# Expert stage with 88 token places instead of 96, and two of sixteen weight blocks as whole 128-column products

## The chip, the cores and the metric

One Trainium2 chip; the kernel runs on one of its cores. The metric is the device time of one execution in microseconds, given as the median of several runs.

## What is computed

The reference is two transformer blocks on 256 tokens of width 1024, all in float32. The part that the change touches is the mixture of experts of the first block's second layer:

```python
def moe_swiglu(h, w_router, w_gate, w_up, w_down):      # h: 256 x 1024
    logits = (h @ w_router).astype(jnp.float32)
    top_val, top_idx = lax.top_k(logits, TOP_K)          # 2 of 8 experts a token
    top_w = jax.nn.softmax(top_val, axis=-1)
    gates = jnp.sum(jax.nn.one_hot(top_idx, N_EXPERTS, dtype=jnp.float32) * top_w[..., None], axis=-2)
    out = jnp.zeros_like(h)
    for e in range(N_EXPERTS):
        y = swiglu(h, w_gate[e], w_up[e], w_down[e])     # 1024 -> 3584 -> 1024
        out = out + gates[..., e:e + 1].astype(h.dtype) * y
    return out
```

Before it stand a gated linear attention, a dense feed forward and a stick-breaking attention; behind it the second block with a gated delta net, convolutional feed forwards and latent attention. None of these is changed.

## The kernel before

**Weights** come as 547 tiles of 1 MiB (128 partitions x 2048 numbers) in the order of their use. SP loads them into `ring`, seven slots; `load_turns` (L160) waits on `tile_used` until the tile seven places earlier has been used, then issues the next transfer. TensorE waits on `landed` of the slot before a tile and adds one to `tile_used` with the tile's last product. All stages share this one stream.

**Routing** (L1195 to L1302). The router's products, top two, softmax; a rank for each token within its expert; `pick`, a 0/1 matrix that gives each chosen token its place among the CAP places of its expert; `place`, which carries gates back to tokens. `flag` (L1254) is set if an expert has more than CAP tokens; then a second path (from L1475), guarded by an If on each engine, computes the experts again for the tokens beyond. It is not entered otherwise.

**Expert stage** (L1304 to L1443), one core, experts in turn. Each expert has 28 gate/up tiles (`nf`) and 14 down tiles (two halves of `kd` = 7), 42 in all, 336 for eight experts. On TensorE, written out by hand in this order:
- for each gate/up tile `s`: wait for the tile, for `moe_hid` (the buffer of two tiles earlier is free), then 2 halves x 8 `k`, each block of 128x128 weights as two products with 64 weight columns, `m` = 0 and 64, that write partitions 0 to 63 and 64 to 127 of the same PSUM columns (L1368). The weights are the stationary side, the expert's CAP tokens (`hTe`) are streamed.
- behind tile 1, `turn` (L1330): eight transposes of the expert before; behind tile 5, `spread_rows` (L1337): four products of 512 columns that add its result to the tokens.
- behind the 28th, `gather` (L1311) of the next expert's tokens: 8 x 2 products, each again as two strips (L1316).
- then the down tiles: 4 `j` x 4 `q` blocks a tile, each as two strips (L1390), CAP tokens of `hid` streamed.

ScalarE takes the silu of each gate/up tile (L1406) when its products are done, VectorE multiplies it with the up half (L1418) into `hid`; VectorE also copies tokens, turned rows and sums. GpSimd copies one 256-wide row set an expert. In float32 one `nc.tensor.matmul` of the program appears in the trace as two pairs of LDWEIGHTS and MATMUL instructions. The page prints L1368 and L1390 for the strip products, L352 and L2316 for products of other stages that are 128 columns wide.

Other lines that the prediction speaks of: L552 and L568 are products of an early stage, L2057, L2061, L2097, L2127 and L2130 of the gated delta net in the second block.

Of the kernel before, what the change touches and what calls it, by code (L numbers as in the profile page):

```python
# [19 lines left out]
P = 128  # L20
D = 1024
KT = D // P
# [10 lines left out]
F_FFN = 2816 // P  # L33
FF = 2816
EPS = 1e-6
CAP = 96
GH = 4
MH = 8
LANES = 4
# [24 lines left out]
def build(nc, stream, params, where, out):  # L64
# [4 lines left out]
    with ExitStack() as ctx:  # L69
# [15 lines left out]
        ps = ctx.enter_context(nc.psum_tensor("ps", [P, 8, 512], F32))  # L85
# [14 lines left out]
        def after_all(eng):  # L100


            for d in everyone:
                n = d.n if len(chain) == 1 else chain[-1].get(d, 0)

                if n and not (len(chain) > 1 and eng.engine == nc.tensor.engine and d in (tile_used, pe_done)):
                    eng.wait_ge(d.sem, n)
# [13 lines left out]
        def link(eng, done, ins):  # L121

            eng.wait_ge(done.sem, done.by(ins))
# [10 lines left out]
        def take(*shape):  # L134
            n = int(np.prod(shape))
            assert cur[0] + n <= ARENA, (cur[0], n)
            v = arena[:, cur[0]:cur[0] + n]
            cur[0] += n
            if len(shape) == 2:
                v = v.rearrange("p (a b) -> p a b", a=shape[0])  # L140
            if len(shape) == 3:
                v = v.rearrange("p (a b c) -> p a b c", a=shape[0], b=shape[1])
            return v
# [5 lines left out]
        @block.sync  # L149
        def _(sp):  # L150

            first = where["first"]
            sp.dma_start(par[:, 0:first], params[:, 0:first]).then_inc(params_in, 16)
            for t in range(RING):
                sp.dma_start(ring[:, t, :], stream[t]).then_inc(landed[t], 16)
            sp.dma_start(par[:, first:width], params[:, first:width]).then_inc(rest_in, 16)
            for t in range(TT):
                sp.dma_start(cx[:, t, :], out["ctx"][t * P:t * P + P, :]).then_inc(rest_in, 16)
# [1013 lines left out]
        finish()  # L1172
        hid = take(F_MOE, CAP)
        sg = take(2, CAP)
        hTe = take(KT, CAP)
        pick = take(TT, EXPERTS, P)
        place = take(EXPERTS + 1, SEQ)
        placed = take(SEQ)
        yT = take(KT, CAP)
        y = take(D)  # L1180
# [69 lines left out]
        def _(dve):  # L1250
            after_all(dve)
            nc.vector.tensor_reduce(over[:, 0:1], ps[:, 4, 16:24], AXX, ALU.max)
            link(dve, dve_done, nc.vector.tensor_copy(rank.rearrange("p t n -> p (t n)"), ps[:, 4, 0:16]))
            link(dve, dve_done, nc.vector.tensor_scalar(flag, over[:, 0:1], float(CAP), None, ALU.is_gt))  # L1254

            link(dve, dve_done, nc.vector.tensor_scalar(rest, rank, float(CAP), None, ALU.is_ge))
            link(dve, dve_done, nc.vector.tensor_tensor(rest, rest, gates, ALU.mult))
# [50 lines left out]
        slot = lambda k: (moe_t0 + k) % RING  # L1308
        wait_of = lambda k: 16 * ((moe_t0 + k) // RING + 1)

        def gather(pe, e):  # L1311

            for k in range(KT):
                for t in range(TT):
                    for m in (0, 64):
                        last = nc.tensor.matmul(ps[m:m + 64, 4 + k // 4, (k % 4) * P:(k % 4) * P + CAP],  # L1316
                                                xn[:, t, k * P + m:k * P + m + 64], pick[:, t, e, 0:CAP],
                                                start=(t == 0), stop=(t == TT - 1), skip_group_check=True)
            last.then_inc(moe_gathered, 1)
# [10 lines left out]
        def turn(pe, e):  # L1330

            pe.wait_ge(moe_sums, e * 2 + 2)
            for k in range(KT):
                last = nc.tensor.transpose(ps[0:CAP, 6 + k // 4, (k % 4) * P:(k % 4) * P + P], yT[:, k, :], ident)
            last.then_inc(moe_turned, 1)

        def spread_rows(pe, e):  # L1337

            pe.wait_ge(moe_y, e + 1)
            pe.wait_ge(moe_place, e + 1)  # L1340
            for half in range(2):
                for t in range(TT):
                    last = nc.tensor.matmul(ps[:, 2 * t + half, :], placed[0:CAP, t * P:t * P + P],
                                            y[0:CAP, half * 512:half * 512 + 512], start=False, stop=False,
                                            skip_group_check=True)
            last.then_inc(moe_spread, 1)
# [5 lines left out]
        @block.tensor  # L1352
        def _(pe):
            after_all(pe)
            gather(pe, 0)
            for e in range(EXPERTS):
                at = e * per

                pe.wait_ge(moe_tokens, e + 1)
                for s in range(nf):  # L1360
                    pe.wait_ge(landed[slot(at + s)], wait_of(at + s))
                    w = ring[:, slot(at + s), :].rearrange("p (k n) -> p k n", k=KT)

                    pe.wait_ge(moe_hid, e * nf + s + 1)
                    for half in range(2):
                        for k in range(KT):
                            for m in (0, 64):
                                last = nc.tensor.matmul(ps[m:m + 64, 4 + s % 2, half * P:half * P + CAP],  # L1368
                                                        w[:, k, half * P + m:half * P + m + 64], hTe[:, k, :],
                                                        start=(k == 0), stop=(k == KT - 1), skip_group_check=True)  # L1370
                    last.then_inc(tile_used.sem, 1)

                    if s == TURN_AT:
                        turn(pe, e)
                    if s == SPREAD_AT:
                        spread_rows(pe, e)

                pe.wait_ge(moe_hid, e * nf + (nf + 2))
                if e + 1 < EXPERTS:
                    gather(pe, e + 1)  # L1380

                for half in range(2):
                    for d in range(kd):
                        k0 = at + nf + half * kd + d
                        pe.wait_ge(landed[slot(k0)], wait_of(k0))
                        w = ring[:, slot(k0), :].rearrange("p (k n) -> p k n", k=4)
                        for j in range(4):
                            for q in range(4):
                                for m in (0, 64):
                                    last = nc.tensor.matmul(ps[m:m + 64, 6 + half, q * P:q * P + CAP],  # L1390
                                                            w[:, j, q * P + m:q * P + m + 64],
                                                            hid[:, 4 * d + j, :], start=(d == j == q == 0),
                                                            stop=(d == kd - 1 and j == 3), skip_group_check=True)
                        last.then_inc(tile_used.sem, 1)
            turn(pe, EXPERTS)
            spread_rows(pe, EXPERTS)
# [1555 lines left out]
```

## Time and profile before

| | us |
|---|---|
| median of 3 runs | 3187.92 (3179.68 to 3188.28) |
| the profiled execution, whole | 3184.05 |
| its span, first to last instruction | 3182.3 |
| TensorE busy with matmuls | 2927.3 (92%) |
| weight loads busy | 2170.5 (68%) |
| VectorE, ScalarE, GpSimd busy | 627.7, 395.5, 36.2 |
| matmuls at L1368 (gate/up), 14336 instructions | 605.6 |
| matmuls at L1390 (down), 7168 instructions | 301.5 |

The profile is of one execution. "PE" is TensorE's matmuls, "PEld" its weight loads, which overlap them; "busy" of a group is the time in which at least one of its instructions ran, so overlapping instructions count once. The mean of one instruction (246 ns at L1368) is longer than the distance from one start to the next, since matmuls are pipelined and two strips run beside each other. Mean granted clock of TensorE over the span is 0.955 of 2.4 GHz. The DMA engines moved 585.60 MB, 580.15 MB of it on the queue of the weight stream.

### The profile page before, as it was taken

Reading aid. Unit: us, or ns where it says so; the run is one execution under the profiler, and the core shown is the slowest. Engines: PE = TensorE matmul, PEld = TensorE weight load, DVE = VectorE, ACT = ScalarE, POOL = GpSimd, SP = SyncE. Lnnn points to the kernel's source line nnn. Section 1 sums busy time; section 2 is a strip of 40 time slices with the busy share of each in tenths; the row PEclk is TensorE's granted clock in tenths of the full one; section 3 lists DMA queues with packets and bytes.
Section 4 is the critical chain, followed back from the end, with each engine's and each line's share of the span. In section 5 each row is a group of like instructions: output and inputs, shape, how many; then the busy total and the mean of one; then the engine's idle time right before and its main releaser. Section 6 shows DMA issues by size and latency. Waiting matters only on the chain. (4 is left out here: it accounts for less than half of the span.)

```text
span 3182.3 us, 70496 instructions
## 1 busy us (share of the span) xinstructions
PE 2927.3 (92%) x31424; PEld 2170.5 (68%) x31424; DVE 627.7 (20%) x1694; ACT 395.5 (12%) x1057; POOL 36.2 (1%) x55
## 2 busy tenths in 40 slices
PE   5889999989999999999996996887999999889999
PEld 2567856669999999999883465774544444545883
DVE  0121001120000000000001124673222210223231
ACT  1000001100000000000002122332111100122210
POOL 0000000000000000000000000000000000000000
PEclk8899999989999999999998987888999999989999
DMA  8774434239999999999991210000222202311342
GB/s 350 306 312 146 146 131 159 106 148 368 364 343 376 368 361 371 366 364 345 345 354 46 68 38 27 2 2 3 77 80 79 79 27 80 132 66 53 133 158 79
DMA packets 80495, 585.60 MB, mean 184 GB/s; under 512 B 8912, under 2 KB 8912, under 8 KB 10064
## 3 DMA queue, kind: packets, MB, share of 16 engines
q1 hardware_dynamic: 79920, 580.15, 48.2%
q8 instruction: 251, 4.11, 0.5%
q10 hardware_dynamic: 288, 1.05, 0.1%
q14 instruction: 36, 0.29, 0.0%
HBM read 580.11 MB, written 1.05 MB: 183 GB/s over the span
## 5 line engine op out<-in xcount | busy, mean ns | idle before, releaser
L1368 PE MATMUL ps<-arena,ring 128*64 128x96 f32 x14336 | 605.6, 246 | 15.0 <-issue 13.0
L1368 PEld LDWEIGHTS ps<-arena,ring 128*64 128x64 f32 x14336 | 595.9, 137 | 28.5 <-issue 26.6
L2316 PE MATMUL ps<-hT,ring 128*128 128x256 f32 (+2 forms) x1472 | 456.8, 473 | 5.6 <-ACT hT L464 3.4
L2316 PEld LDWEIGHTS ps<-hT,ring 128*128 128x128 f32 x1472 | 276.0, 192 | 185.2 <-issue 166.3
L352 PE MATMUL ps<-ring,arena 128*128 128x512 f32 x896 | 388.4, 594 | 4.4 <-DVE small L1595 3.3
L352 PEld LDWEIGHTS ps<-ring,arena 128*128 128x128 f32 x896 | 170.4, 191 | 216.5 <-issue 214.9
L1390 PE MATMUL ps<-arena,ring 128*64 128x96 f32 x7168 | 301.5, 246 | 7.3 <-issue 6.6
L1390 PEld LDWEIGHTS ps<-arena,ring 128*64 128x64 f32 x7168 | 297.5, 137 | 10.5 <-issue 8.9
L198 PE MATMUL ps<-hT,ring 128*128 128x256 f32 (+1 forms) x672 | 223.7, 494 | 10.4 <-ACT arena L749 4.0
L198 PEld LDWEIGHTS ps<-hT,ring 128*128 128x128 f32 x672 | 130.2, 195 | 101.1 <-issue 91.6
L1418 DVE TENSOR_TENSOR arena<-arena,ps 128x96 f32<-128x96 f32 x224 | 56.9, 254 | 584.0 <-ACT arena L1406 584.0
L1406 ACT ACTIVATE arena<-ps 128x96 f32<-128x96 f32 x224 | 56.1, 250 | 884.1 <-PE ps L1368 884.1
L923 PE MATMUL ps<-hT,ring 128*128 128x256 f32 (+1 forms) x736 | 152.7, 370 | 2.6 <-ACT hT L462 2.6
L923 PEld LDWEIGHTS ps<-hT,ring 128*128 128x128 f32 x736 | 134.8, 190 | 20.3 <-issue 3.0
L2361 DVE SCALAR_TENSOR_TENSOR arena<-ps,par,arena 128x510 f32<-128x510 f32 (+1 forms) x88 | 50.1, 611 | 300.3 <-ACT arena L2349 300.3
L213 PE MATMUL ps<-ring,hT 128*128 128x512 f32 (+1 forms) x224 | 95.8, 587 | 0.0
L568 PE MATMUL ps<-ring,arena 128*32 128x256 f32 x768 | 51.0, 425 | 37.1 <-DMA ring<-in_stream 37.1
L2349 ACT ACTIVATE arena<-ps,par 128x512 f32<-128x512 f32 (+1 forms) x88 | 46.3, 576 | 278.7 <-PE ps L2316 278.7
L213 PEld LDWEIGHTS ps<-ring,hT 128*128 128x128 f32 x224 | 43.0, 194 | 51.2 <-issue 47.1
L386 DVE TENSOR_TENSOR arena<-ps,arena 128x512 f32<-128x512 f32 x24 | 16.6, 692 | 261.6 <-PE ps L352 210.6
L1429 DVE COPY arena<-ps 128x384 f32<-128x384 f32 x16 | 8.9, 558 | 295.3 <-PE ps L1390 295.3
L568 PEld LDWEIGHTS ps<-ring,arena 128*32 128x32 f32 x768 | 27.2, 122 | 55.6 <-issue 43.9
(498 smaller groups left out, 2228.5 us busy)
## 6 DMA issues: line engine op xcount, KB each, us to landing
ring<-in_stream SPq DMA_DIRECT2D x547, 1024.0 KB, 6.1
par<-in_params SPq DMA_DIRECT2D x1, 3397.0 KB, 28.8
h<-in_x ACTq DMA_DIRECT2D x2, 512.0 KB, 8.0
cx<-in_ctx SPq DMA_DIRECT2D x2, 512.0 KB, 29.5
out<-h SPq DMA_DIRECT2D x4, 256.0 KB, 2.0
par<-in_params SPq DMA_DIRECT2D x1, 941.0 KB, 6.1
```

Of the source, the lines that this page charges most:

```text
L198: last = nc.tensor.matmul(o[:, 0:ntok], w[:, k, half * P:half * P + P], src[:, k, tok0:tok0 + ntok], start=(k == 0), stop=(k == KT - 1))
L213: last = nc.tensor.matmul(ps[:, b, 0:cols], src[:, k, tok0 + n * P:tok0 + n * P + P], w[:, k - t0, 0:cols], start=(k == 0), stop=(k == kti ...
L352: last = nc.tensor.matmul(ps[:, b, :], src[:, k, t * P:t * P + P], w[:, k % kper, :], start=(k == 0), stop=(k == ktiles - 1))
L568: last = nc.tensor.matmul(ps[32 * j:32 * j + 32, 7, 0:256], cond[:, k, :], w, start=(k == 0), stop=(k == KT - 1))
L923: last = nc.tensor.matmul(ps[:, b, half * SEQ + tok.start:half * SEQ + tok.stop], w[:, k, half * P:half * P + P], hT[:, k, tok], start=(k ...
L1368: last = nc.tensor.matmul(ps[m:m + 64, 4 + s % 2, half * P:half * P + CAP], w[:, k, half * P + m:half * P + m + 64], hTe[:, k, :], start=( ...
L1390: last = nc.tensor.matmul(ps[m:m + 64, 6 + half, q * P:q * P + CAP], w[:, j, q * P + m:q * P + m + 64], hid[:, 4 * d + j, :], start=(d == ...
L1406: nc.scalar.activation(sg[:, s % 2, :], ps[:, 4 + s % 2, 0:CAP], ACT.Silu).then_inc(moe_silu, 1)
L1418: nc.vector.tensor_tensor(hid[:, s, :], sg[:, s % 2, :], ps[:, 4 + s % 2, P:P + CAP], ALU.mult).then_inc(moe_hid, 1)
L2316: last = nc.tensor.matmul(ps[:, 2 * BANKS_CONV[f % RING] + half, tok], w[:, k, half * P:half * P + P], hT[:, k, tok], start=(k == 0), stop ...
L2349: nc.scalar.activation(buf[:, b, :], ps[:, 2 * b + half, 0:ntok], ACT.Copy, scale=tap(1, half, f)).then_inc(conv_centre, 1)
L2361: nc.vector.scalar_tensor_tensor(seg(o, 1, SEQ), seg(x, 0, SEQ - 1), tap(0, half, f), seg(o, 1, SEQ), ALU.mult, ALU.add).then_inc(conv_lef ...
```

## The change

CAP, the number of token places of an expert, goes from 96 to 88. Every buffer, product and copy that is CAP wide narrows with it. In the gate/up tiles and the down tiles, block 7 and block 8 of the sixteen (in the order in which a tile's blocks are multiplied) become one product each with 128 weight columns, written to all 128 partitions; the other fourteen stay two strips of 64. In a gate/up tile these are the last `k` of the first half and the first `k` of the second; in a down tile `j` = 1, `q` = 3 and `j` = 2, `q` = 0. `gather` keeps its strips.

```diff
-CAP = 96
+CAP = 88
+WHOLE = (7, 8)
...
+        def strips(n):
+
+            return [(0, P)] if n in WHOLE else [(0, 64), (64, P)]
+
...
                     for half in range(2):
                         for k in range(KT):
-                            for m in (0, 64):
-                                last = nc.tensor.matmul(ps[m:m + 64, 4 + s % 2, half * P:half * P + CAP],
-                                                        w[:, k, half * P + m:half * P + m + 64], hTe[:, k, :],
+                            for a, b in strips(k + half * KT):
+                                last = nc.tensor.matmul(ps[a:b, 4 + s % 2, half * P:half * P + CAP],
+                                                        w[:, k, half * P + a:half * P + b], hTe[:, k, :],
                                                         start=(k == 0), stop=(k == KT - 1), skip_group_check=True)
...
                         for j in range(4):
                             for q in range(4):
-                                for m in (0, 64):
-                                    last = nc.tensor.matmul(ps[m:m + 64, 6 + half, q * P:q * P + CAP],
-                                                            w[:, j, q * P + m:q * P + m + 64],
+                                for a, b in strips(4 * j + q):
+                                    last = nc.tensor.matmul(ps[a:b, 6 + half, q * P:q * P + CAP],
+                                                            w[:, j, q * P + a:q * P + b],
                                                             hid[:, 4 * d + j, :], start=(d == j == q == 0),
                                                             stop=(d == kd - 1 and j == 3), skip_group_check=True)
```

## Rows read from the trace of the kernel before

**Rows 1.** The page: span, busy time, and its 40 slices of the span (tenths)
```profile
span 3182.3 us, 70496 instructions
...
PE 2927.3 (92%) x31424; PEld 2170.5 (68%) x31424; DVE 627.7 (20%) x1694; ACT 395.5 (12%) x1057; POOL 36.2 (1%) x55
...
PEclk8899999989999999999998987888999999989999
DMA  8774434239999999999991210000222202311342
```

**Rows 2.** Two experts as stretches: us, busy of each engine, PEclk, DMA share, GB/s
```profile
1175.00:1294.00 119.00, 118.37 (x2760) 115.51 (x2758) 10.47 (x33) 7.00 (x28) 0.40 (x1) 1.00 0.95 370
...
1418.00:1545.00 127.00, 120.61 (x2771) 116.46 (x2768) 10.47 (x33) 7.00 (x28) 0.40 (x1) 1.00 0.92 351
```

**Rows 3.** Waits (total us, times, longest): TensorE's in the expert stage, then SP's queue's own
```profile
PE ps L1368 <- issue: 13.0, 20, 1.4
PE ps L1390 <- issue: 4.6, 10, 1.3
...
SPq L166 <- PE ps L1368: 563.0, 224, 45.0
```

**Rows 4.** Timeline of ScalarE, 1174 to 1200 us: start, duration, instruction, [idle before]
```profile
1177.91 0.25 ACT L1406 ACTIVATE arena<-ps 128x96 f32<-128x96 f32 x1 [2.39 <-PE ps L1368]
1181.71 0.25 ACT L1406 ACTIVATE arena<-ps 128x96 f32<-128x96 f32 x1 [3.55 <-PE ps L1368]
1184.35 0.25 ACT L1406 ACTIVATE arena<-ps 128x96 f32<-128x96 f32 x1 [2.39 <-PE ps L1368]
...
1189.63 0.25 ACT L1406 ACTIVATE arena<-ps 128x96 f32<-128x96 f32 x1 [2.39 <-PE ps L1368]
1196.06 0.25 ACT L1406 ACTIVATE arena<-ps 128x96 f32<-128x96 f32 x1 [6.17 <-PE ps L1368]
```

**Rows 5.** Groups by line and form: count, busy us, mean ns, idle before
```profile
L1368 PE MATMUL ps<-arena,ring 128*64 128x96 f32 x14336 | 605.6, 246 | 15.0 <-issue 13.0 <-DVE arena L1325 1.1
...
L352 PE MATMUL ps<-ring,arena 128*128 128x512 f32 x896 | 388.4, 594 | 4.4 <-DVE small L1595 3.3 <-DVE small L1596 1.1
L1390 PE MATMUL ps<-arena,ring 128*64 128x96 f32 x7168 | 301.5, 246 | 7.3 <-issue 6.6 <-DVE arena L1418 0.6
```

**Rows 6.** Timeline of TensorE, 64x64 products with 64 columns, 1989.3 to 1990.2 us
```profile
1989.54 0.31 PE L2127 MATMUL ps<-par 64*64 64x64 f32 x4
...
1990.01 0.31 PE L2127 MATMUL ps<-arena 64*64 64x64 f32 x4
```

**Rows 7.** Timeline of TensorE around the turn at L1334, 809.2 to 811 us
```profile
808.96 0.66 PE L1368 MATMUL ps<-arena,ring 128*64 128x96 f32 x11
809.55 1.08 PE L1334 MATMUL ps<-par,arena 128*96 128x128 f32 x8
810.56 0.63 PE L1368 MATMUL ps<-arena,ring 128*64 128x96 f32 x10
```

**Rows 8.** L2057 by itself: duration ns min/median/max
```profile
L2057 PE MATMUL ps<-par,hT x64: 218/218/267, 1975.3 to 2146.6; 64*64 64x64 f32 x64
```

**Rows 9.** Timeline of TensorE, strips, four whole products of 128 columns, strips
```profile
1975.25 0.45 PE L2057 MATMUL ps<-par,hT 64*64 64x64 f32 x8 [1.62 <-issue]
1975.63 0.71 PE L2061 MATMUL ps<-hT,arena 128*128 128x128 f32 x4
1976.27 0.45 PE L2097 MATMUL ps<-arena 64*64 64x64 f32 x8
```

**Rows 10.** Timeline of TensorE, four whole products of 8 columns, then strips
```profile
198.95 0.61 PE L552 MATMUL ps<-par,arena 128*128 128x8 f32 x4
199.49 0.42 PE L568 MATMUL ps<-ring,arena 128*32 128x256 f32 x4
```

**Rows 11.** Two other stretches, columns as in rows 2: of the expert stage, of small products
```profile
1200.00:1300.00 100.00, 99.30 (x2376) 98.57 (x2374) 8.92 (x27) 5.51 (x22) 0.00 (x0) 1.00 0.97 381
1950.00:2150.00 200.00, 160.35 (x2362) 145.78 (x2364) 134.20 (x519) 67.89 (x236) 0.00 (x0) 0.84 0.01 2
```

## The prediction

> **What bounds the kernel now.** I read the page first. The span is 3182.3 us and TensorE works in 92% of it; in the slices of the expert stage (10 to 21) its clock and the DMA engines both stand at 9 tenths [rows 1]. Two candidates for the bound, so the page can't decide. By stage, two whole experts take 119 and 127 us at full clock with the DMA engines 92 to 95% busy [rows 2]. The waits decide: TensorE's largest wait in the stage is "issue", 13.0 and 4.6 us, and no wait for `ring<-in_stream` is listed, while SP's queue waited 563.0 us in 224 waits for the products of L1368 [rows 3]. The weights are there early and the ring is full, so **TensorE's own pace bounds the stage**. That pace is read off the silu, which follows each gate/up tile: 2.64 us apart (1181.71, 1184.35) [rows 4]. A tile is 16 blocks of 128x128, each as two 64-column strips; a strip product is two MATMUL instructions (14336 for 224 tiles [rows 5]), and the two strips run beside each other, so a tile is 32 starts of a pair, 2.64/32 = 82.5 ns each. The stage has 8 x 42 = 336 tiles, down tiles of the same form (7168 instructions for 112 tiles [rows 5]). One nanosecond a tile is 0.336 us of the kernel. "Same" below means within 0.3%, about 10 us, what a measurement of this kernel can tell from no change.
>
> **Narrower strips (CAP 96 to 88).** Where 64 columns are streamed, four groups of four MATMULs (two pair starts each) begin between 1989.54 and 1990.01, 58.8 ns a start [rows 6]. Between 58.8 at 64 and 82.5 at 96 a straight line gives 76.6 at 88; by cycles, 82.5 ns is 198 of 2.4 GHz, two for each of 96 columns and 6 over, so 88 columns make 182 cycles, 75.8 ns. I take 76. Bounds: 75.8, and 82.5 if the pace doesn't follow the columns; the row of 58.8 shows that four instructions can be issued in less, so I lean to the lower end. All 16 blocks in strips would be 32 x 76 = 2.43 us.
>
> **Two whole blocks in the middle.** Blocks 7 and 8 are neighbours in both loops, so a tile is strips, four MATMUL instructions with 128 weight columns, strips. The trace has no such run with 88 columns, but it has its pieces from both sides:
> - From the last strip start to the first whole one: the strips at L1368 end at 808.96 + 0.66 = 809.62, the last began 0.246 earlier [rows 5], at 809.37, and L1334 begins at 809.55 [rows 7]: 176 ns where 82.5 is normal. With 64 columns it is 1975.25 + 0.45 - 0.218 = 1975.48 (L2057) to 1975.63 (L2061), 0.15 us [rows 8, 9]. So TensorE runs empty first: two cycles a column and some 96 ns. At 88 columns: 73 + 96 = 169 ns.
> - From the first of four whole MATMULs to the next strips: 0.54 us with 8 columns (198.95 to 199.49) [rows 10] and 0.64 us with 128 (1975.63 to 1976.27) [rows 9]. That is four weight loads of some 0.11 us in a row, the last product's two cycles a column and again about 97 ns of emptying: 437 + 7 + 97 = 541 and 437 + 107 + 97 = 641. At 88: 437 + 73 + 97 = 607 ns.
> - From the first strips to the second: after L1334 five starts lie within 810.56 + 0.63 - 0.246 - 810.56 = 0.384 us [rows 7], less three of 82.5 it is 136 ns with 96 columns, because the first load isn't hidden. At 88: 127 ns.
> - The tile has 32 starts still, 26 of them at 76: 26 x 76 + 169 + 607 + 127 = **2.88 us**, against 2.64. The whole blocks cost 0.45 us and the narrower strips give 0.21.
>
> A second reading of the same price: the turn at L1334 lengthens a tile from 2.64 to 3.80 us (1177.91 to 1181.71) [rows 4]. By the pieces it is 176 + 1010 + 134 - 2 x 82.5 = 1155 ns [rows 7], which closes. Eight spread instructions of 512 columns at the 434 ns of L352 (388.4 us for 896) are 3.47, and the tile with them takes 6.43 [rows 4, 5]: 0.32 us for both switches. Four whole products at 111 ns (a quarter of 437, plus 2) with 28 starts at 76 and 0.29 to 0.36 for the two switches is 2.86 to 2.93 us. Those are my bounds for the tile. These switches happen twice in an expert now; the change makes one round trip in each of 336 tiles.
>
> **The skill's rule against the rows.** The strip that leaves ends before the whole one starts, in each of the rows above. The Trainium skill, "TensorEngine Tiling (Array Packing)", Key Properties, has that as a rule: changing the tiling mode drains TensorE. By that rule the change pays 672 drains; the trace agrees, with 96 ns each beyond the columns.
>
> **Other terms.** Gather (L1316, 32 strip products of two instructions, 32 pair starts an expert) narrows by 6.5 ns a start: 8 x 32 x 6.5 = -1.7 us. Turn and spread keep their streamed 128 and 512 columns: nothing. The loads at L1334 narrow from 96 to 88 columns under products of 128: hidden. L1406 waits 2.39 us a tile for TensorE [rows 4] and L1418 follows it, so what they save is off the path. Stalls on "issue": 13.0 and 4.6 us [rows 3], and experts of 119 and of 127 us show them [rows 2]. DMA engines have less to do per microsecond (1 MiB in 2.88 us instead of 2.64) and TensorE asks for 120 instructions a tile instead of 128, over a longer time. Bounds 0 and -18; I take half, -9, and this is the softest term. No DMA, wait or queue is moved: SP's waits on `tile_used` come once a tile as before, 0.24 us later each, and nothing queues behind a new wait since none is added. Its cover, the full ring, only grows.
>
> **Sum.** 336 x 0.24 = +80.6, -1.7, -9: **+70 us**. The profiled execution took 3184.05 us (its span [rows 1] and 1.8 us around it), which would become 3254; it is 3.9 us under the median 3187.92 of the runs shown, so the forecast of the median is 3258.
>
> **Rivals.**
> - *Loads overlap better at 88 columns.* If the array can start on the first whole product while its weights still load, one exposed load of 0.11 us a tile goes: tile 2.77, +70 - 37 = +33, 3221. Against it: 0.54 us for four products of only 8 columns says the four loads follow each other anyway [rows 10]. Chance 0.12. The Trainium skill, "TensorE: Matmul & The Clock Gate", Architectural detail, states that a MATMUL can begin before its LDWEIGHTS completes; that is this rival's ground, and no row here shows it saving time at a switch.
> - *The other side: the switch is free.* If the whole block's weights load behind running strips, so that nothing empties (the emptyings above would then belong to L1334's and L552's own waits), a tile is 28 x 76 + 4 x 111 = 2.57 us, -0.07 x 336 = -23, with the gather -25, and the median 3163. It decides where the two switches together cost under 0.07 us, against the 0.29 to 0.36 above. Against it: L2057 to L2061 is one block of instructions without a wait between, and shows 0.15 as well [rows 8, 9]. The DMA engines wouldn't stop it: at the 381 GB/s and 97% busy of one stretch [rows 11] a tile lands every 2.75 us, 2.67 at 100%, and with turn (1.16), spread (3.79) and gather (32 starts, 2.6) in each 42 tiles TensorE would ask for one every 2.75. Chance 0.06.
> - *The strips don't get faster.* Then 26 x 6.5 = 0.17 us a tile comes back, +57: 3315. Against it stand [rows 6]. Chance 0.05.
> - *The clock falls.* Granted clock was 1.00 in both experts and 0.84 where small products alternate with waits [rows 2, 11]. Emptying the array twice a tile leaves TensorE at work most of the time; if a tenth of the tiles ran at the lower level (1.2 GHz), some 34 x 2.8 = +95 us more. Chance 0.04.
> - *The change sends tokens over the cap.* An expert with more than 88 tokens sets `flag` and the whole stage is done again by the second path, roughly another 900 us. 512 places over 8 experts are 64 on average, and the reference's router gives its fullest expert 75. Chance 0.01.
>
> **How the numbers follow.** The forecast has 0.72. Its own range: 336 x 0.22 - 1.7 - 18 = +54 to 336 x 0.29 - 1.7 = +96, 3242 to 3284. Taken down past the first rival, 3215 to 3285 holds about 0.83. Faster is the free switch and 0.01 for what isn't listed: 0.07. Same needs a tile within 0.03 us of 2.64 after the stalls, which lies between the cases: 0.04. Slower is the rest, 0.89.
>
> **What would show it.** In the changed profile: silu 2.88 us apart in ordinary tiles; strips 76 ns a start; MATMULs with 128 weight columns and 88 streamed, 896 of them at the gate/up line and 448 at the down line; 0.17 us before the first and 0.61 from it to the next strips; experts of about 130 us; DMA nearer 340 GB/s; clock 1.00. Wrong would be: silu 2.57 apart (free switch), 2.77 (loads overlap), 3.05 (strips as slow as now), a clock under 1.00 in the stage, or TensorE waiting for `ring<-in_stream`.

## The result, and the profile after

The changed kernel takes **3228.17 us** (median of 4 runs, 3217.01 to 3231.88) against 3183.8 us for the kernel before (4 runs): ratio 1.0144, 95% interval 1.0096 to 1.0192, so 44 us or 1.4% slower. The forecast was slower by 70 us, 3258, with a range of 3215 to 3285. Sign, mechanism and the stated range held; the size came out more than a third smaller than forecast. The two profiled executions, 3184.05 and 3227.55 us, are 43.5 us apart, and everything below is about them.

Span and busy time of the changed kernel, as in [rows 1], and then two stretches of the length of an expert (us, busy of PE, PEld, DVE, ACT, POOL, PEclk, DMA share, GB/s):

```profile
span 3225.8 us, 67808 instructions
...
PE 2995.2 (93%) x30080; PEld 2182.7 (68%) x30080; DVE 624.8 (19%) x1694; ACT 394.0 (12%) x1057; POOL 36.2 (1%) x55
```

```profile
1201.00:1330.00 129.00, 128.38 (x2598) 117.56 (x2596) 10.12 (x33) 6.81 (x28) 0.40 (x1) 1.00 0.91 343
1072.00:1201.00 129.00, 128.38 (x2600) 117.56 (x2596) 10.11 (x33) 6.81 (x28) 0.40 (x1) 1.00 0.92 343
```

An expert takes 129.3 us now, and seven of the eight agree to 0.2 us (the last has no gather behind it); before, the eight took 119.6 to 128.2 us. The clock is 1.00, and the DMA engines moved 343 GB/s. The silu of each gate/up tile, from the timeline of ScalarE, begins here at an expert's second tile, with the turn behind it; the spread stands behind the sixth (1216.91):

```profile
1204.23 0.24 ACT L1411 ACTIVATE arena<-ps 128x88 f32<-128x88 f32 x1 [2.64 <-PE ps L1373]
1208.27 0.24 ACT L1411 ACTIVATE arena<-ps 128x88 f32<-128x88 f32 x1 [3.80 <-PE ps L1373]
1211.15 0.24 ACT L1411 ACTIVATE arena<-ps 128x88 f32<-128x88 f32 x1 [2.64 <-PE ps L1373]
...
1216.91 0.24 ACT L1411 ACTIVATE arena<-ps 128x88 f32<-128x88 f32 x1 [2.64 <-PE ps L1373]
1223.58 0.24 ACT L1411 ACTIVATE arena<-ps 128x88 f32<-128x88 f32 x1 [6.42 <-PE ps L1373]
```

From 1208.27 to 1211.15 is **2.88 us, the forecast tile** (2.64 before [rows 4]). The groups by form show the four whole instructions a tile, 896 at the gate/up line and 448 at the down line, and what the strips became (to set beside [rows 5]):

```profile
L1373 PE MATMUL ps<-arena,ring 128*64 128x88 f32 x12544 | 530.0, 241 | 1.0 <-DVE arena L1330 1.0
...
L1373 PE MATMUL ps<-arena,ring 128*128 128x88 f32 x896 | 151.9, 292 | 0.0
...
L1395 PE MATMUL ps<-arena,ring 128*128 128x88 f32 x448 | 76.0, 292 | 0.0
```

What surprises is in the column behind the last bar. TensorE's idle time before L1368 was 15.0 us, 13.0 of it "issue" [rows 5]; before L1373 it is 1.0, and none of it is issue. From 682 us, just behind the start of the stage, to its end TensorE's whole list of waits (total us, times, longest) is this, and SP's queue still waits for TensorE in 224 waits, as in [rows 3]:

```profile
PE ps L1321 <- DVE arena L1423: 4.4, 7, 0.6
PE ps L1395 <- DVE arena L1423: 0.6, 1, 0.6
```

```profile
SPq L167 <- PE ps L1373: 593.3, 224, 45.0
```

TensorE adds one to `tile_used` at the end of each tile, so the stage can be added up from these 336 times in the trace. Every ordinary tile of the changed kernel takes 2.883 us; of the kernel before, most take 2.640 and some 60 take up to 1.6 us more.

| 335 steps of the stage, us | before | after | difference |
|---|---|---|---|
| 335 ordinary tiles | 884.4 | 965.8 | +81.4 |
| turn, spread, gather beyond a tile | 66.0 | 63.3 | -2.7 |
| tiles longer than the ordinary one ("stalls") | 33.6 | -0.2 | -33.8 |
| sum | 984.0 | 1028.9 | +44.9 |

Ahead of the stage and behind it the two profiles differ by 1.3 and 0.3 us. So the change cost 81 us, and took away 34 us of stalls with it. The experiments ask whether the 81 us are made as the prediction had it, and what the stalls are.

### The profile page after: what moved, and what is told of

Same layout as the page of the kernel before. It is cut to its first block and busy times, and to the rows that moved or that the text cites. A ratio compares the mean times of both kernels' runs of the same rounds, so it can differ in the third digit from the quotient of the medians.

```text
span 3225.8 us, 67808 instructions
## 1 busy us (share of the span) xinstructions
PE 2995.2 (93%) x30080; PEld 2182.7 (68%) x30080; DVE 624.8 (19%) x1694; ACT 394.0 (12%) x1057; POOL 36.2 (1%) x55
## 5 line engine op out<-in xcount | busy, mean ns | idle before, releaser
L1373 PE MATMUL ps<-arena,ring 128*64 128x88 f32 (+1 forms) x13440 | 650.6, 244 | 1.0 <-DVE arena L1330 1.0
L1373 PEld LDWEIGHTS ps<-arena,ring 128*64 128x64 f32 (+1 forms) x13440 | 604.0, 140 | 51.7 <-issue 7.5
L1395 PE MATMUL ps<-arena,ring 128*64 128x88 f32 (+1 forms) x6720 | 324.2, 244 | 0.6 <-DVE arena L1423 0.6
L1395 PEld LDWEIGHTS ps<-arena,ring 128*64 128x64 f32 (+1 forms) x6720 | 301.9, 140 | 22.3 <-DVE arena L1423 0.8
L1423 DVE TENSOR_TENSOR arena<-arena,ps 128x88 f32<-128x88 f32 x224 | 55.1, 246 | 617.3 <-ACT arena L1411 617.3
L1411 ACT ACTIVATE arena<-ps 128x88 f32<-128x88 f32 x224 | 54.5, 243 | 931.7 <-PE ps L1373 931.7
L924 PEld LDWEIGHTS ps<-hT,ring 128*128 128x128 f32 x736 | 134.8, 190 | 20.3 <-issue 3.0
L1434 DVE COPY arena<-ps 128x352 f32<-128x352 f32 x16 | 8.4, 524 | 312.3 <-PE ps L1395 312.3
```

Source lines behind the costliest of these rows:

```text
L924: last = nc.tensor.matmul(ps[:, b, half * SEQ + tok.start:half * SEQ + tok.stop], w[:, k, half * P:half * P + P], hT[:, k, tok], start=(k ...
L1373: last = nc.tensor.matmul(ps[a:b, 4 + s % 2, half * P:half * P + CAP], w[:, k, half * P + a:half * P + b], hTe[:, k, :], start=(k == 0), s ...
L1395: last = nc.tensor.matmul(ps[a:b, 6 + half, q * P:q * P + CAP], w[:, j, q * P + a:q * P + b], hid[:, 4 * d + j, :], start=(d == j == q == ...
L1411: nc.scalar.activation(sg[:, s % 2, :], ps[:, 4 + s % 2, 0:CAP], ACT.Silu).then_inc(moe_silu, 1)
L1423: nc.vector.tensor_tensor(hid[:, s, :], sg[:, s % 2, :], ps[:, 4 + s % 2, P:P + CAP], ALU.mult).then_inc(moe_hid, 1)
```

## The experiments

Each kernel ran on one chip beside the kernel before; ratios are to that, with 95% intervals. "Stalls" is always the third line of the table above, from the same semaphore times. The cuts of code are edits of the changed kernel where nothing else is said. One caution for differences of a few us: the stages behind this one, whose code and loads are the same in all kernels but the two with shorter packets, took 1497 to 1511 us from one profiled execution to another.

### One half of the change: narrower strips alone

```diff
-WHOLE = (7, 8)
+WHOLE = ()
```

> CAP 88, all sixteen blocks of a tile in strips: the change without its whole blocks. Theory A (the two switches a tile are the loss): TensorE's own tile falls to 32 x 76 = 2.43 us, 336 tiles give -70 us against the kernel before, gather -1.7; but then the weights land no faster than one tile in about 2.67 us, so the stage ends nearer 336 x 2.67 = 897 us against 951 with the stalls of before, and TensorE should now wait for ring<-in_stream or stall on issue: total about 3110 to 3140. Theory B (the stalls on issue grow with the pace and eat the gain): total within 15 us of before, with over 60 us of stalls. If neither the narrower strips nor the whole blocks matter, no change from the kernel of the change, 3228.

Measured: 3195.51 us (5 runs), before 3181.9, ratio 1.0054 (1.0021 to 1.0087). **Without the whole blocks the narrower strips gain nothing.** The ordinary tile did fall, to 2.427 us, but the stage took 986.0 us against 984.0, since the stalls rose from 33.6 to 106.3. The time is even 14 us longer, but of the 7 us between the two profiled executions 5.5 lie behind the stage, in code that is the same; that loss isn't explained by the stalls. Four silus in a row, and TensorE's waits:

```profile
731.32 0.24 ACT L1411 ACTIVATE arena<-ps 128x88 f32<-128x88 f32 x1 [3.39 <-PE ps L1373]
733.75 0.24 ACT L1411 ACTIVATE arena<-ps 128x88 f32<-128x88 f32 x1 [2.18 <-PE ps L1373]
738.51 0.24 ACT L1411 ACTIVATE arena<-ps 128x88 f32<-128x88 f32 x1 [4.51 <-PE ps L1373]
742.09 0.24 ACT L1411 ACTIVATE arena<-ps 128x88 f32<-128x88 f32 x1 [3.33 <-PE ps L1373]
```

```profile
PE ps L1373 <- issue: 58.5, 63, 2.3
PE ps L1395 <- issue: 21.6, 27, 1.4
```

One tile takes 2.43, the next 4.76, the next 3.58. It isn't the weights that are late: in the whole stage each tile had landed at least 7.6 us before TensorE began it (7.7 in the kernel before; half of them over 10), and no wait for `ring<-in_stream` is listed. Theory B of this run holds. What is late, as this and the next experiments show, is TensorE's code. The page of each kernel has a queue for instructions, here that of this kernel, which is the same in the kernel before, and that of the changed one:

```profile
q8 instruction: 251, 4.11, 0.5%
...
q8 instruction: 239, 3.92, 0.5%
```

251 packets of 16 KB. The changed kernel has 2688 TensorE instructions fewer and 12 packets fewer, and the kernel with four whole blocks below 5376 and 21 fewer: a packet holds some 256 of TensorE's instructions, two tiles' worth of 128. At 2.43 us a tile one would be wanted every 4.9 us. From 700 to 1600 us one comes every 5.7 us on average, in this kernel as in the one before. The stalls follow these packets. Of 89 distances of more than 0.25 us from one matmul start to the next within L1373 or L1395 in that stretch, 88 end between 1.2 and 1.7 us after an instruction packet has ended (median 1.41); before, all of 34 do (median 1.38). By chance it would be one in eleven. The Trainium skill, "Runtime: NRT & Kernel Launch", Instruction fetch mechanics, says that code comes in 16 KiB blocks of 256 instructions by a DMA queue of the engine's own, and that crossing a block is mostly hidden. The block size agrees; "mostly hidden" doesn't hold here, where it costs 34 to 106 us.

### The other half: whole blocks alone, at 96

```diff
-CAP = 88
+CAP = 96
```

> CAP stays 96, blocks 7 and 8 whole: the other half of the change alone. Pieces by the columns: 26 starts of 82.5, 176 into the whole block, 187 + 112 + 112 + 205 over it, 134 behind it = 3.07 us a tile, +0.43 x 336 = +145 us, less about 35 of stalls that should be gone as in the changed kernel: about +110, 3294. If the whole blocks were only dear together with 88 columns it would stay under 3230.

Measured: 3294.23 us (4 runs), ratio 1.0367 (1.0338 to 1.0397). The tile is 3.08 us, and the stalls are -0.1:

```profile
739.80 0.25 ACT L1411 ACTIVATE arena<-ps 128x96 f32<-128x96 f32 x1 [2.82 <-PE ps L1373]
742.88 0.25 ACT L1411 ACTIVATE arena<-ps 128x96 f32<-128x96 f32 x1 [2.83 <-PE ps L1373]
```

The whole blocks are a loss of 0.44 us a tile in this kernel too, so they aren't dear for want of 96 columns.

### Are the switches the price, or the whole products?

```diff
-WHOLE = (7, 8)
+WHOLE = (4, 11)
```

> CAP 88, two whole blocks but apart (blocks 4 and 11): the same products as the change, four switches a tile instead of two. If the switch is the price (it empties the array): 24 x 76 + 2 x (169 + 180 + 205 + 127) = 3.19 us a tile against 2.88, +103 us over the changed kernel, about 3331. If the price lies in the whole products' weight loads and not in the switch, the tile stays at 2.88 and the time at 3228.

Measured: 3333.53 us (4 runs), ratio 1.049 (1.0459 to 1.052). The same products in two places instead of one: 3.20 us a tile (3.19 expected), 105 us over the changed kernel.

```profile
744.62 0.24 ACT L1411 ACTIVATE arena<-ps 128x88 f32<-128x88 f32 x1 [2.95 <-PE ps L1373]
747.81 0.24 ACT L1411 ACTIVATE arena<-ps 128x88 f32<-128x88 f32 x1 [2.95 <-PE ps L1373]
```

**A pair of switches costs 0.31 us a tile** (3.195 - 2.883), by itself more than the 0.21 that the narrower strips give.

The products by themselves are priced by two more whole blocks beside the others:

```diff
-WHOLE = (7, 8)
+WHOLE = (6, 7, 8, 9)
```

> CAP 88, blocks 6 to 9 whole: twice the whole products of the change, the same two switches a tile. From the changed kernel's own starts: 22 pair starts of 76, 169 into the whole blocks, 180, six of 112, 205 out and 127 = 3.02 us a tile, +0.14 x 336 = +48 over the changed kernel, 3276. If the loss of the change were all in the switches, the tile would stay at 2.88 and the time at 3228.

Measured: 3273.4 us (2 runs), ratio 1.0275 (1.0219 to 1.0331). The tile is 3.026 us: two more whole blocks cost 0.143 us, 72 ns each, with no further switch. Of the changed kernel's 0.456 us over a tile of strips (2.883 - 2.427), 0.14 is therefore in the products and 0.31 in the switches.

```profile
743.42 0.24 ACT L1411 ACTIVATE arena<-ps 128x88 f32<-128x88 f32 x1 [2.78 <-PE ps L1373]
746.45 0.24 ACT L1411 ACTIVATE arena<-ps 128x88 f32<-128x88 f32 x1 [2.78 <-PE ps L1373]
```

### What makes the stalls go: fewer instructions, or the pace?

```diff
-CAP = 96
+CAP = 104
```

> CAP 104, all blocks in strips: as many TensorE instructions a tile as before (128) at a pace near that of the changed kernel, 32 x 89 = 2.85 us a tile. It asks what made the 33 us of stalls on issue go. If the pace (instructions and DMA bytes per microsecond) decides, the stalls are gone here too: +0.21 x 336 = +71, gather +2, stalls -33: about +40, 3224. If the smaller number of instructions (120 a tile with whole blocks) decides, the stalls stay at 20 us or more: 3245 to 3260.

Measured: 3220.23 us (4 runs), ratio 1.0134 (1.0106 to 1.0163). Edited in the kernel before: 128 instructions a tile as there, and a tile of 2.853 us. The stalls are 1.0 us, and no "issue" is left in TensorE's waits of the stage. The slower pace is enough; the saved instructions aren't needed for it. (A slower pace asks for both fewer instructions and fewer weight bytes per microsecond; the next experiment takes these apart.)

```profile
743.62 0.26 ACT L1406 ACTIVATE arena<-ps 128x104 f32<-128x104 f32 x1 [2.60 <-PE ps L1368]
746.47 0.26 ACT L1406 ACTIVATE arena<-ps 128x104 f32<-128x104 f32 x1 [2.60 <-PE ps L1368]
```

### Is it the code by itself, or the weights beside it?

```diff
-            load_turns(sp, 1, moe_turn)
+            load_turns(sp, 1, 17)
+            load_turns(sp, 17, 64, TILE // 2)
+            load_turns(sp, 64, moe_turn)
```

The first run makes this edit in the kernel before, the second in the changed kernel with `WHOLE = ()`. `load_turns` copies only the first `cols` columns of a tile, here half of them; the rest of the slot keeps older weights, so these kernels leave out half of the stage's weights and their output is not the reference's. TensorE's instructions are untouched; the DMA engines carry half the bytes, in as many packets of half the size.

> The kernel before (CAP 96, strips), but the weight tiles of the expert stage from the seventh on load only the first half of their columns, so the DMA engines carry half the bytes there; the second half of the ring slot keeps older weights, and the output is that of other weights. TensorE's instructions are the same in number and pace. Theory A (TensorE stalls because its instruction fetch shares the DMA engines with the weights): the 33.6 us of lengthened tiles in the stage fall under 5, total about 3150. Theory B (fetching 256 instructions takes some 5.3 us by itself, whatever the other traffic, and 2 tiles of 2.64 us ask for them at just that pace): the stalls stay at 25 to 35, total about 3183.

> The same half loads, with CAP 88 and all blocks in strips (tile 2.43 us, stalls 106 us with full loads). Theory A: the stalls fall under 15 us, and the total comes to about 3184 - 70 - 34 + 10 = 3090. Theory B: two tiles still take about 5.3 us or more, stalls of 70 us or more, total 3160 to 3195.

Measured: 3150.01 us (2 runs), ratio 0.9898 (0.9869 to 0.9928), with stalls of 0.5 us; and at 88 places 3080.2 us (2 runs), ratio 0.9679 (0.9649 to 0.9709), with stalls of 10.3 instead of 106.3. Theory A holds in both. The stretch from 700 to 1600 us of the first (columns as above), and what is left of "issue" in the second:

```profile
700.00:1600.00 900.00, 894.90 (x20863) 873.27 (x20863) 78.90 (x253) 54.50 (x218) 3.20 (x8) 1.00 0.58 188
```

```profile
PE ps L1395 <- issue: 3.8, 6, 0.9
PE ps L1373 <- issue: 1.3, 4, 0.6
```

TensorE can run at 2.43 us a tile; **its code arrives late because of the 360 GB/s of weights beside it**. The instruction packet itself takes 0.95 us with full and with half loads alike, so it is its start that comes late; when it was asked for, the trace doesn't show.

### Shorter packets

```diff
-                    sp.dma_start(ring[:, s, :], stream[turn * RING + s]).then_inc(landed[s], 16)
+                    for c0 in (0, TILE // 2):
+                        sp.dma_start(ring[:, s, c0:c0 + TILE // 2],
+                                     stream[turn * RING + s][:, c0:c0 + TILE // 2]).then_inc(landed[s], 16)
```

The first run makes this edit in the kernel before, with the waits on `landed` doubled to match; the second again has 88 places and strips alone.

> The kernel before, each weight tile loaded by two transfers of half its columns, so packets of 4 KB instead of 8 KB. If the instruction packet waits behind a weight packet in progress on each engine, shorter packets let it in sooner: stalls from 33 to under 20 us, total 3165 to 3175. If 4 KB packets move fewer bytes per second, or waiting isn't by packets, the total is the same or higher, 3180 to 3200.

> The same two transfers a tile, with CAP 88 and all blocks in strips. If shorter packets free the instruction fetch, this is the version that could beat the kernel before: stalls from 106 to 60 us or less, total 3150 or less. If not, 3195 as with whole transfers or above it.

Measured: 3264.83 us (4 runs), ratio 1.0271 (1.0227 to 1.0315), and at 88 places 3260.81 us (4 runs), ratio 1.0237 (1.0208 to 1.0265). A miss: the hope was wrong, and even the second reading, 3180 to 3200, fell short by 65 us. The engines are 94% busy and move 331 GB/s where 8 KB packets made 360 at the same share, and "issue" before the gate/up and down lines grows from 19.6 to 77.3 us (first run):

```profile
700.00:1600.00 900.00, 823.62 (x18612) 788.67 (x18609) 70.26 (x225) 48.29 (x193) 2.80 (x7) 1.00 0.94 331
```

```profile
PE ps L1371 <- issue: 56.1, 60, 3.1
PE ps L1393 <- issue: 21.2, 29, 1.4
```

By the semaphore times the stalls are 114 us, and 172 at 88 places. Again no wait for weights is listed, and each tile had landed at least 7.4 us ahead. The stage takes 1065.7 us with tiles of 2.64 and 1058.1 with tiles of 2.43: as with 8 KB packets (984.0 and 986.0), TensorE's own pace hardly matters any more, and the time is that of 172 instruction packets, now one every 6.2 us. Fewer bytes per second and more packets make the stalls worse, which points at the DMA engines' time as what runs short, rather than at the bytes that the memory gives; no run takes these two apart by itself. That agrees with the half loads, from the other side.

### Between the two kernels

If a pace of 2.64 has 34 us of stalls and one of 2.88 none, the best lies between. Two ways there: whole blocks in every second tile alone, and, in the kernel before, `CAP = 100`, all in strips.

```diff
-        def strips(n):
+        def strips(n, tile):
-            return [(0, P)] if n in WHOLE else [(0, 64), (64, P)]
+            return [(0, P)] if n in WHOLE and tile % 2 else [(0, 64), (64, P)]
```

> CAP 88, blocks 7 and 8 whole in every second tile alone: tiles of 2.43 and 2.88 us in turn, 2.655 on average with 124 TensorE instructions, so an instruction packet (256 of them) is wanted every 5.5 us instead of 5.3. Fetch theory: stalls between the 34 us of before and 0 of the changed kernel, about 10 to 20, and the stage 335 x 2.655 + 63 + 15 = 968 against 984: total about 3168, the version that could beat both. If the average rate at which weights land is the bound instead, the stage stays at 984 and the total at 3184.

> CAP 100, all strips: tile 32 x 85.8 = 2.745 us, 128 instructions, a packet wanted every 5.49 us, about as often as with whole blocks in every second tile, but by an even pace. Fetch theory: stalls of 5 us or less, stage 335 x 2.745 + 67 + 5 = 992, total about 3191. If pace and instruction count together don't decide the stalls, they stay above 15 us and the total above 3200.

Measured: **3168.48 us** (12 runs), before 3183.75 (23 runs), ratio **0.9950 (0.9930 to 0.9971)**: faster than the kernel before by 15 us, half a percent, and than the changed one by 60. Its silus come 2.43 and 2.88 us apart in turn, and of "issue" in the stage this is left:

```profile
707.57 0.24 ACT L1411 ACTIVATE arena<-ps 128x88 f32<-128x88 f32 x1 [2.64 <-PE ps L1373]
710.00 0.24 ACT L1411 ACTIVATE arena<-ps 128x88 f32<-128x88 f32 x1 [2.18 <-PE ps L1373]
712.88 0.24 ACT L1411 ACTIVATE arena<-ps 128x88 f32<-128x88 f32 x1 [2.64 <-PE ps L1373]
```

```profile
PE ps L1395 <- issue: 5.7, 12, 1.0
PE ps L1373 <- issue: 5.3, 9, 1.3
PE ps L1321 <- issue: 0.2, 1, 0.2
```

Its stage is 973.3 us with 20.4 of stalls, where 968 was expected; that is 11 us less than before, and the rest of the 15 lies outside the stage, where the edit changes nothing. With 100 places: 3186.01 us (12 runs), ratio 1.0003 (0.9982 to 1.0025), no change that can be measured; tile 2.747, stalls 2.7.

All kernels with whole weight transfers side by side, from the same readings:

| kernel | ordinary tile, us | instructions a tile | stalls, us | stage, us |
|---|---|---|---|---|
| strips, 88 | 2.427 | 128 | 106.3 | 986.0 |
| before (strips, 96) | 2.640 | 128 | 33.6 | 984.0 |
| every second tile, 88 | 2.655 (mean) | 124 | 20.4 | 973.3 |
| strips, 100 | 2.747 | 128 | 2.7 | 988.6 |
| strips, 104 | 2.853 | 128 | 1.0 | 1023.2 |
| the change | 2.883 | 120 | -0.2 | 1028.9 |
| four whole blocks, 88 | 3.026 | 112 | -0.1 | 1076.9 |
| whole blocks, 96 | 3.076 | 120 | -0.1 | 1095.3 |
| whole blocks apart, 88 | 3.195 | 120 | 0.0 | 1133.6 |

Below some 2.7 us a tile, what is taken off the products comes back as stalls; above it each nanosecond counts in full. The every-second version and the kernel before have nearly the same mean pace, yet 13 us less of stalls; whether the 4 instructions fewer a tile do this, or the chance of one profile, wasn't tried apart. That the version is faster rests on its timed runs.

## Why the prediction was right, and where its size was off

- **The bound.** TensorE's own pace: right. With the tile 0.24 us longer SP still waits for TensorE, and the experiments that lengthen the tile moved the time by just that.
- **Narrower strips, 76 ns a start.** Measured 2.427/32 = 75.8 in the run with strips alone. Right, at the lower end of the bounds.
- **Into the whole block, 169 ns.** Measured 169, the median of 336.
- **Four whole products to the next strips, 607 ns.** Measured 609 (starts 180, 112 and 112 apart, then 205). The sum was right and the picture behind it loose: it had four loads of some 110 in a row, where the first distance is 180 and only the next two are 112.
- **Back to strips, 127 ns.** Measured 127. Together 2.88 us a tile forecast, 2.883 measured; +80.6 forecast and +81.4 measured. The bounds 2.86 to 2.93 held, and three more kernels came out within 0.01 us of a tile put together from the same pieces.
- **The price of the switch** decided the sign. The run with the blocks apart shows it by itself: 0.31 us a tile for two more switches. The rule of the Trainium skill that the prediction names beside it ("TensorEngine Tiling (Array Packing)", Key Properties: changing the tiling mode drains TensorE) gives the same sign and no price. One sentence there misreads the rows: the leaving strip doesn't end before the whole product starts, by the ends shown it ends 0.07 us after (809.62 against 809.55 in [rows 7], 1975.70 against 1975.63 in [rows 9]). These ends are modelled, and what the rows do show is the longer distance between starts.
- **Gather and turn.** Forecast -1.7, measured -1.6 for gather (25.4 to 23.8, seven of the eight) and -1.0 for the turn, where a stall had been.
- **Stalls on "issue".** Here the size failed. The step took half of the 17.6 us of idle time [rows 3], -9, with -18 as its bound; all 33.8 went. There were three errors in it. The waits were read up to 1640 us and the stage lasts to 1669; the whole of it lists 20.3 us. The waits give only time in which TensorE stood idle, and matmuls are pipelined, so a gap between starts shows there by some 0.16 us too little (246 ns of one instruction less 82.5), and short ones not at all: 33.6 us of lengthened tiles showed as 20.3. The experts had it, 119.6 against up to 128.2 us. And half was a middle value with no mechanism behind it; the stalls end between 2.64 and 2.75 us a tile, as the runs with 100 and 104 places show. The range that the sum had of its own, 3242 to 3284, was missed by this; 3228 lies in the stated one only because that was taken down to 3215 for a rival that didn't come about, which is luck. With -33.8 for -9 the sum is +70 - 25 = +45, which is what the profiles show. Of the 30 us between 3258 and 3228, this step is 25; 4 more are the median of the kernel before, 3187.92 in the forecast and 3183.8 beside the changed kernel.
- **The rivals.** None came about: the switch isn't free (169 and 205 ns stand in each tile), the strips did get faster, the clock stayed at 1.00, no second path was entered, and no exposed load went, though the time came near that rival's 3221 for another reason. A reader of the times alone would have taken the wrong case. The rival of the free switch was also priced too fast: it had tiles of 2.57 us and no more stalls than before, where tiles of 2.43 us lost all that they gained; a tile of 2.57 with these weights wasn't run.

## What to carry to other kernels

Cost a change of an engine's instruction form by the starts on both sides of the same switch elsewhere in the trace: here pieces from a transpose and from two groups of products in other stages gave the tile to within 0.01 us. Read "issue" idle time as a term of its own, measure it as the lengthening of otherwise equal steps rather than by idle time, and ask what it depends on before halving it. And where an engine's long straight code and a stream of weights share the DMA engines, a faster inner loop may gain nothing until the code's share is cheaper: look for the pace at which the stalls begin.

## What the hardware showed that was not expected

- TensorE's instruction packets (16 KB, 0.95 us each) come late beside the weights: at 358 GB/s and a packet wanted every 4.9 us, 106 us of stalls in a stage of 986; at half the weight bytes and the same code, 10.
- The stall ends some 1.4 us after the packet has ended, not at its end (median 1.41, 88 of 89 stalls between 1.2 and 1.7).
- Transfers in 4 KB packets moved 331 GB/s with the DMA engines 94% busy, against 360 with 8 KB packets at the same share.
- When the array goes from 64-column strips to a product of 128 weight columns and back, each of the two switches has its price: 169 ns from the last strip start to the first whole one, and 205 from the last whole start to the next strip, where 76 and 112 are the ordinary steps. That the array runs empty in them is how the prediction has it; the starts alone don't show it.
